# Experts in column strips: plain fp32 matmuls without a weight split, room for 96 rows an item, seven weight buffers

## The reference

```python
def swiglu(h, w_g, w_u, w_d):
    return (jax.nn.silu(h @ w_g) * (h @ w_u)) @ w_d

def moe_swiglu(h, w_router, w_g, w_u, w_d):
    t = h.reshape(-1, D_MODEL)
    logits = (t @ w_router).astype(jnp.float32)
    top_v, top_i = lax.top_k(logits, TOP_K)            # TOP_K = 2
    top_w = jax.nn.softmax(top_v, axis=-1)
    gate = jnp.sum(jax.nn.one_hot(top_i, N_EXPERTS, dtype=jnp.float32) * top_w[..., None], axis=1)
    for e in range(N_EXPERTS):                          # 8
        out = out + gate[:, e:e + 1] * swiglu(t, w_g[e], w_u[e], w_d[e])
```

## Time and profile before

| | before |
|---|---|
| median of 3 runs | 1993.19 us (1988.62 to 1993.28) |
| profiled execution | 1991.17 us |
| its span (first to last instruction) | 1989.4 us |
| mean granted clock of PE | 0.975 of full |
| PE busy | 1855.9 us (93%) |
| DVE busy | 1404.4 us (71%) |
| ACT busy | 1136.1 us (57%) |
| HBM read | 521.81 MB, 263 GB/s over the span |

### The profile page before, as it was taken

One profiled execution on the slowest core, in us unless ns is written; L12 is line 12 of the kernel. 1 busy time (PEld: TensorE's weight loads), 2 busy tenths in 40 slices (PEclk: granted clock), 3 DMA queues, 4 the chain that ended last, 5 costly groups with the idle time before them and its releaser, 6 DMA issues.

```text
span 1989.4 us, 28834 instructions
## 1 busy us (share of the span) xinstructions
PE 1855.9 (93%) x10925; PEld 1581.4 (79%) x10925; DVE 1404.4 (71%) x1711; ACT 1136.1 (57%) x1391; POOL 91.9 (5%) x105
## 2 busy tenths in 40 slices
PE   4999998999978899988999999999999999999997
PEld 2799888888866799986777777787777777777776
DVE  1477575434425577757888888888888788788885
ACT  2455544333323445525777767767777777777774
POOL 3010031000000100210000000000000000000000
PEclk8999998999998999988999999999999999999998
DMA  9364674677673444434989988989899899898993
GB/s 323 108 218 170 223 272 139 243 254 254 245 263 126 165 138 168 148 110 144 358 324 329 359 327 323 359 298 350 329 329 350 335 325 351 302 355 328 330 351 127
DMA packets 229738, 524.62 MB, mean 264 GB/s; under 512 B 5156, under 2 KB 11506, under 8 KB 229664
## 3 DMA queue, kind: packets, MB, share of 16 engines
q1 hardware_dynamic: 227456, 519.72, 72.5%
q0 software_dynamic: 2208, 3.85, 0.8%
HBM read 521.81 MB, written 1.74 MB: 263 GB/s over the span
## 4 chain that ended last, share of the span: by engine, by line
PE 60%; DVE 16%; DMA 9%; ACT 7%; issue 6%; POOL 1%; ACTq 0%; DVEq 0%; SPq 0%; POOLq 0%
PE ps L1380 18%; PE ps L1382 16%; PE ps L1381 16%; DVE wlo L1335 9%; ACT whi L807 4%; DMA raw<-in_w_ff_down_dram 3%; PE ps L1386 3%; DMA raw<-in_w_e_gate_dram 2%; DMA raw<-in_w_e_down_dram 2%; DVE wlo L857 2%; PE ps L1753 2%; PE ps L1441 1%; DMA raw<-in_w_ada_dram 1%; ACT whi L545 1%; PE ps L1775 1%
## 5 line engine op out<-in xcount | busy, mean ns | idle before, releaser
L1335 DVE TENSOR_TENSOR wlo<-raw,whi 128x1024 fp32r<-128x1024 f32 x672 | 780.5, 1220 | 115.2 <-ACT whi L807 115.2
L807 ACT ACTIVATE whi<-raw 128x1024 fp32r<-128x1024 f32 x672 | 669.4, 1053 | 38.8 <-PE ps L1382 38.7
L1380 PE MATMUL ps<-whi,hT_hi 128*128 128x512 f32 (+2 forms) x1024 | 407.6, 398 | 30.8 <-DVE wlo L1335 12.1
L857 DVE TENSOR_TENSOR wlo<-raw,whi 128x1024 fp32r<-128x1024 f32 (+1 forms) x220 | 266.8, 1247 | 218.2 <-ACT whi L545 218.0
L1381 PE MATMUL ps<-wlo,hT_hi 128*128 128x512 f32 (+2 forms) x1024 | 393.3, 384 | 0.0
L1382 PE MATMUL ps<-whi,hT_lo 128*128 128x512 f32 (+2 forms) x1024 | 392.8, 384 | 0.0
L1380 PE MATMUL ps<-hT_hi,whi 128*128 128x256 f32 x1248 | 361.6, 290 | 19.6 <-DVE hT_lo L902 8.4
L1381 PE MATMUL ps<-hT_lo,whi 128*128 128x256 f32 x1248 | 355.6, 285 | 0.0
L1382 PE MATMUL ps<-hT_hi,wlo 128*128 128x256 f32 x1248 | 355.4, 285 | 0.0
L545 ACT ACTIVATE whi<-raw 128x1024 fp32r<-128x1024 f32 (+1 forms) x220 | 222.0, 1049 | 119.3 <-PE ps L1382 45.6
L1380 PEld LDWEIGHTS ps<-whi,hT_hi 128*128 128x128 f32 x1024 | 194.0, 189 | 102.7 <-DVE wlo L1335 50.4
(11 more groups left out here) (269 smaller groups left out, 1779.7 us busy)
## 6 DMA issues: line engine op xcount, KB each, us to landing
raw<-in_w_e_gate_dram SPq DMA_DIRECT2D x56, 2048.0 KB, 7.8
raw<-in_w_e_up_dram SPq DMA_DIRECT2D x56, 2048.0 KB, 7.8
raw<-in_w_e_down_dram SPq DMA_DIRECT2D x56, 2048.0 KB, 7.7
raw<-in_w_ada_dram SPq DMA_DIRECT2D x24, 2048.0 KB, 10.6
raw<-in_w_in_dram SPq DMA_DIRECT2D x22, 2048.0 KB, 9.0
raw<-in_w_ff_gate_dram SPq DMA_DIRECT2D x7, 2048.0 KB, 7.7
raw<-in_w_ff_up_dram SPq DMA_DIRECT2D x7, 2048.0 KB, 7.9
raw<-in_w_ff_down_dram SPq DMA_DIRECT2D x7, 2048.0 KB, 8.1
```

Of the source, the lines that this page charges most:

```text
L807: act.activation(h, part, ACT.Copy).then_inc(hi_piece, 1)
L857: tt(w, part, h.bitcast(F32), ALU.subtract).then_inc(lo_piece, 1)
L1335: tt(w, part, h.bitcast(F32), ALU.subtract).then_inc(lo_piece, 1)
L1380: mm(out, a_hi, b_hi, start=start, stop=False, skip_group_check=shared)
```

## The change

The dense part stays as it is, but for the place of its tiles in SBUF. The four arrays `whi`, `wlo`, `acts_hi` (once `hT_hi` and `br_hi`) and `acts_lo` are given back after it, and four more weight buffers (`e_raw`) lie there. So the experts have seven buffers (E_SLOTS), the three of `raw` and these four.

In an item there is no split. The gathered tokens (`xe`) and the turned hidden tile (`hidT`) are plain fp32, and PE reads the weights where the DMA put them. An item has room for 96 rows (CAP = 96). Its tokens are the stationary operand in strips of 32: three strips hold the three groups of 32 tokens for one k-tile. The fourth strip does another share of the same chunk: the last four k-tiles of up for each group in turn (`UP_PARTS`), and in down the k-tiles 2 and 3 of the second output half (`Y_PARTS`). Its sums stand in partitions 96 to 127 of three banks. ACT moves each to its group's rows (`moved`), and DVE adds them.

With 96 rows a second level is needed: an expert may need two extra items (LEVELS = 2), and the table, its constants (now loaded by POOL behind the router's weights, `rconsts`) and the number of possible items grow (OVER from 3 to 5). The count alone is written first (`count_done`), so that PE and ACT need not wait for the whole table. Up is loaded ahead of gate.

```diff
-CAP = 128
+CAP = 96
+LEVELS = 2
 OVER = 512 // (CAP + 1)
...
+E_SLOTS = 7
+E_LOADS = [("up", 0), ("gate", 0)]
+for _c in range(1, CHUNKS):
+    E_LOADS += [("up", _c), ("gate", _c), ("down", _c - 1)]
+E_LOADS.append(("down", CHUNKS - 1))
...
+        e_raw = sb("e_raw", [P, E_SLOTS - RAW, 2 * HALF])
...
+            def given_back(j, i):
+                kind, ch = E_LOADS[j]
+                if kind == "down":
+                    sp.wait_ge(down_done, i * CHUNKS + (ch + 1))
+                else:
+                    sp.wait_ge(gu_done, i * (3 * CHUNKS) + (3 * ch + (3 if kind == "up" else 2)))
...
+                    if j >= E_SLOTS:
+                        given_back(j - E_SLOTS, i)
+                    elif not first:
+                        given_back(j - E_SLOTS + len(E_LOADS), i - 1)
+                    elif j < RAW:
+                        s = len(SLOTS) - RAW + j
+                        sp.wait_ge(lo_piece, 2 * (FIRST_HALF[s] + SLOTS[s][3]))
+                    elif j == RAW:
+                        sp.wait_ge(piece_used, 2 * HALVES)
...
+            pool.dma_start(rconsts, shape_consts[:, K_KEPT:K_COLS]).then_inc(router_in, 16)
...
+            def moved(dst, t, bank):
+                return act.activation(dst[32 * t:32 * t + 32, :], ps[CAP:P, bank, :], ACT.Copy)
             with act.Fori(0, n_items) as i:
-                        act.activation(h, part, ACT.Copy).then_inc(hi_piece, 1)
...
+                for ch in range(CHUNKS):
+                    for t in range(3):
+                        act.wait_ge(gu_done, i * (3 * CHUNKS) + (3 * ch + t + 1))
+                        if t == 1:
+                            act.activation(e_gate, ps[0:CAP, B_GATE, :], ACT.Silu)
+                        ins = moved(up_part, t, UP_PARTS[t])
+                    ins.then_inc(up_parted, 1)
+                    if ch == CHUNKS - 1:
+                        keep_gathered(i + 2)
+                    act.wait_ge(e_turn, i * CHUNKS + (ch + 1))
+                    act.activation(hidT[:, ch % 2, :, :].rearrange("p k s -> p (k s)"), ps[:, B_TURN, 0:4 * CAP],
+                                   ACT.Copy).then_inc(e_kept, 1)
...
+                act.wait_ge(down_done, i * CHUNKS + CHUNKS)
+                for t in range(3):
+                    moved(y_part, t, Y_PARTS[t])
+                act.activation(y_tok[:, 0:512], ps[0:CAP, B_Y, :], ACT.Copy).then_inc(y_parted, 1)
...
             with dve.Fori(0, n_items) as i:
-                        tt(w, part, h.bitcast(F32), ALU.subtract).then_inc(lo_piece, 1)
...
+                for ch in range(CHUNKS):
+                    dve.wait_ge(up_parted, i * CHUNKS + (ch + 1))
+                    tt(e_hidden, ps[0:CAP, B_UP, :], up_part, ALU.add).then_inc(up_sum, 1)
+                    dve.wait_ge(up_sum, i * CHUNKS + (ch + 1))
+                    tt(e_hidden, e_hidden, e_gate, ALU.mult).then_inc(e_hid, 1)
...
+            def gate_up(ch, i):
+                wu = landed("up", ch, i)
+                wg = landed("gate", ch, i)
+                for r in range(12):
+                    if r == 8 and ch:
+                        pe.wait_ge(e_kept, i * CHUNKS + ch)
+                    for t in range(3):
+                        if r < 8:
+                            mm(strip(B_GATE, t), tokens(r, t), wg[:, r, :], start=(r == 0), stop=(r == 7))
+                        else:
+                            mm(strip(B_UP, t), tokens(r - 8, t), wu[:, r - 8, :], start=(r == 8), stop=(r == 11))
+                    t, k = divmod(r, 4)
+                    ins = mm(strip(UP_PARTS[t], 3), tokens(4 + k, t), wu[:, 4 + k, :], start=(k == 0), stop=(k == 3))
+                    if k == 3:
+                        ins.then_inc(gu_done, 1)
...
+            def down(ch, i):
+                pe.wait_ge(e_kept, i * CHUNKS + (ch + 1))
+                wd = landed("down", ch, i)
...
+                for r in range(6):
+                    n, k = divmod(r, 4)
+                    if r == 4 and not last:
+                        turn_hidden(ch + 1, i)
+                    for t in range(3):
+                        mm(strip(B_Y + n, t), hidden(k, t), wd[:, k, 512 * n:512 * n + 512],
+                           start=first and k == 0, stop=last and k == (1 if n else 3))
+                    t, k = divmod(r, 2)
+                    ins = mm(strip(Y_PARTS[t], 3), hidden(2 + k, t), wd[:, 2 + k, 512:1024],
+                             start=first and k == 0, stop=last and k == 1)
+                ins.then_inc(down_done, 1)
...
             with pe.Fori(0, n_items) as i:
+                pe.wait_ge(xe_kept, i + 1)
+                for ch in range(CHUNKS):
+                    gate_up(ch, i)
+                    if ch == 0:
+                        scatter(i)
+                        turn_hidden(0, i)
+                    else:
+                        if ch == CHUNKS - 1:
+                            pe.wait_ge(selT_kept, i + 2)
+                            gather(i + 2)
+                        down(ch - 1, i)
+                down(CHUNKS - 1, i)
+            scatter(n_items)
```

More of the change, by code:

```diff
@@ L352, in piece_views @@
                 k, w, part = 1, 1024, whole[:, n:n + 1, :]
-            elif kind in ("tok", "na_qk") or item:
+            elif kind in ("tok", "na_qk"):
                 k, w, part = 2, width, whole[:, 2 * n:2 * n + 2, :]
@@ L357, in piece_views, with e_load @@
             return (part,) + tuple(x[:, buf, 0:k * w].rearrange("p (k n) -> p k n", k=k) for x in (whi, wlo))
[L359 to L367, removed]
-            return piece_views(kind, 0, hh % 2, c_, (len(SLOTS) + hh // 2) % RAW,
-                               (2 * (HALVES + hh) + c_) % PIECES, item=True)
+        def e_load(kind, ch):
+            j = E_LOADS.index((kind, ch))
+            k = 4 if kind == "down" else 8
+            return j, e_slot[j % E_SLOTS].rearrange("p (k n) -> p k n", k=k)
         def filled(l, f):
@@ L1765, in scatter, with strip, landed @@
-            def scatter(hh, i):
-                for r, bank in I_SCATTER[hh]:
-                    if r == 0:
-                        pe.wait_ge(y_kept, i + 1)
-                        pe.wait_ge(selT_kept, i + 1)
-                    if r == 3:
-                        pe.wait_ge(item_added, i * 4 + 1)
+            def strip(bank, t):
+                return ps[32 * t:32 * t + 32, bank, :]
+            def landed(kind, ch, i):
+                j, w = e_load(kind, ch)
+                pe.wait_ge(e_landed[j % E_SLOTS], i * (16 * len(E_LOADS) // E_SLOTS) + 16 * (j // E_SLOTS + 1))
+                return w
@@ new lines, in turn_hidden, with hidden @@
+            def turn_hidden(ch, i):
+                pe.wait_ge(e_hid, i * CHUNKS + (ch + 1))
+                for k in range(4):
+                    ins = turn(ps[:, B_TURN, CAP * k:CAP * k + CAP], e_hidden[:, P * k:P * k + P])
+                ins.then_inc(e_turn, 1)
+            def down(ch, i):
+                pe.wait_ge(e_kept, i * CHUNKS + (ch + 1))
+                wd = landed("down", ch, i)
+                first, last = ch == 0, ch == CHUNKS - 1
+                def hidden(k, t):
+                    return hidT[:, ch % 2, k, 32 * t:32 * t + 32]
+                if first:
+                    pe.wait_ge(item_added, i * 4 + 4)
+                for r in range(6):
[9 more added lines that the diff above has]
+                ins.then_inc(down_done, 1)
@@ L1773, in scatter @@
+            def scatter(i):
+                pe.wait_ge(y_kept, i + 1)
+                pe.wait_ge(selT_kept, i + 1)
+                for r in range(4):
                     for jj in range(2):
                         j = 2 * r + jj
-                        ins = mm(ps[:, bank, NT * jj:NT * jj + NT], y_tok[:, P * j:P * j + P], selT, start=True,
-                                 stop=True)
+                        ins = mm(ps[:, SCATTER_BANKS[r], NT * jj:NT * jj + NT], y_tok[:, P * j:P * j + P], selT,
+                                 start=True, stop=True)
```

316 lines of the change are left out of this document (118 added, 198 removed).

## The result

The changed kernel takes 2065.3 us (median of 4 runs, 2061.72 to 2068.94), the kernel before 1991.81 us in the same comparison. The ratio is 1.0371, 95% interval 1.0348 to 1.0395: 3.7% slower. 2032 was forecast; 2065.3 lies in the range, 33 us above the point. The profiled execution took 2061.72 us for a span of 2059.9.

The account below looks back on a forecast made before the run. PE was taken as the bound, with little slack in DMA. Start 914.4, nine items of 121.5 and end 20.8 gave a span of 2028.7 us, 2032 as median; range 2010 to 2088, chance 0.80.

Parts of the forecast that it names:

- Nine items: Expert stage: expert 0's 111 tokens exceed 96, so nine items run in place of eight, the ninth at full cost, 121.5 us.
- Strips, 108.4 us an item: PE in gate, up and down: 126 rounds of four strips at 0.86 us each, against 114.2 us for the split form.
- Turns, gather, scatter: PE's other work in an item: seven hidden-tile turns 4.6 us, gather 3.1, scatter 3.4, select-matrix turns 0.3.
- Left-over waits and drains: PE's remaining idle time in an item, shown by no row: between 0 and 6.9 us, taken as 1.7.
- DVE, ACT and the handoff: Item: DVE some 15 us, ACT some 25, neither bounds; 2.0 us handoff before PE's turn hidden with 1.4 to spare.
- DMA: Expert weight loads: 5.78 us each at 363 GB/s, ending at 1983 us, before PE's 2008, so costing nothing.
- one of the signs: Expected observation in the expert stage's profile: DMA share above 0.95.
- The late-load rival: Expert stage: late loads at 340 GB/s cost 45 us; with late handoffs 2060 to 2110 us, joint chance 0.16.
- Start, 914.4: Expert stage's first item starts at 914.4 us, with 2 us added for late router weights and constants, 2 for low clock.
- the 2 us for a low clock: Stage start: first matmuls run at 1.2 GHz after the sparse selection, adding 2 us.
- End: After the last item: three strip copies, one copy and an add replace one copy, 20.8 us in place of 18.7.
- Sum: Whole kernel: 914.4 + 9 x 121.5 + 20.8 = 2028.7 us span, 2030.5 profiled, 2032 as median.

Follow-up runs that it names:

- e2: Changed kernel with an extra item only above 128 tokens, so no ninth item and 15 tokens of expert 0 left out: 1940.39 us, ratio 0.9746.
- e9: Kernel before with items of 96 rows in place of 128, so nine items, weight split kept: 2125.05 us, ratio 1.0654.
- e1: Changed kernel with PE's first seven items written out and the last two in a loop, one taken jump left: 2027.88 us, ratio 1.0183.
- e12: Changed kernel with PE's items written out, expert 0's item with 128 rows, no ninth item: 1937.05 us, ratio 0.9710 against the kernel before.
- e5: Changed kernel with six rounds of each chunk's gate and up left out, all loads kept, 1530 instructions between jumps: 1926.25 us.
- e7: Kernel before with gate and up matmuls cut into two of 256 columns, 1936 instructions in the body: 2043.08 us.
- e8: Kernel before with gate, up and down matmuls cut into two of 256 columns, 2272 instructions in the body: 2057.34 us.
- e11: Changed kernel with three weight buffers in place of seven: 2603.88 us.
- e10: Changed kernel with expert loads after the first item's bringing only 32 columns, PE working on stale weights: 2029.65 us.

## Why the prediction was right on the sign and low by 33 us

- **Nine items**: right, and it decides the sign. e2 and e9 price it alone, 125 us with strips and 132 without.
- **Strips, 108.4 us an item**: right. Passes start 0.43 us apart throughout at full clock, and 500.00 of 500 us are busy where no jump lies (e1, e12).
- **Turns, gather, scatter**: forecast 4.6 + 0.3, 3.1 and 3.4 us. In the item from 1160.90 to 1286.60 us, groups by line (busy, mean ns):

```profile
L1396 PE MATMUL ps<-consts,big 96*128 96x96 f32 (+1 forms) x30 | 4.2, 259 | 0.0
L1763 PE MATMUL ps<-big 128*128 128x96 f32 x32 | 3.8, 277 | 0.0
L1841 PE MATMUL ps<-big 96*128 96x256 f32 x16 | 3.7, 386 | 0.0
```

  The gather costs what it did with 128 columns: its upper bound was the right one. The three make 11.7 us, and 11.4 had been put down for them. One reading behind them was wrong: the 0.21 us that I took for a drain between tiling modes is the length of a pass (0.63 us long, started 0.43 apart), with no switch near it. A switch from strips to the scatter costs 0.14 us here, the scatter starting 0.57 us after the last pass:

```profile
1048.80 0.63 PE L1798 MATMUL ps<-raw,KTt 128*32 128x512 f32 x3
...
1049.37 3.72 PE L1841 MATMUL ps<-big 96*128 96x256 f32 x16
```

- **The step that failed: "Left-over waits and drains", 1.7 us.** I looked there for waits on data. Within an item next to nothing is left: 120.33 us an item without a jump (e12), 0.2 more than strips and the three groups above, and 1.2 below the forecast. What I left out was no wait on data but the loop's own jump: 125.74 - 120.33 = 5.4 us at each of eight boundaries, 43.5 us in all. Its 0.2 us stood in the trace of before, as a row of the sequencer, and I took for granted that a longer body does not change it. The text on the change counted matmuls, four for a round in place of three for a k-tile, but priced only their time on the array.
- **DVE, ACT and the handoff**: right. No turn waits for `e_hid` in the stage.
- **DMA**: hidden, as forecast, but priced too high at 363 GB/s. Windows of 10 us show more:

```profile
1100.00:1110.00 10.00, 10.00 (x96) 2.99 (x92) 0.00 (x0) 2.21 (x4) 0.00 (x0) 1.00 1.04 402
```

  and e5 held 394 GB/s. The readings of the earlier trace rows were what three buffers asked for, not what DMA can do. It is also why one of the signs did not come: the DMA share of an item is 0.94, where I wanted it above 0.95. The Trainium skill (DMA: Bandwidth & Descriptors, Specifications) gives about 358 GB/s as a core's limit, one of two equal shares of a stack's 716; here one core loads alone, the 402 and 394 are above that share, and the measurement decides. The late-load rival rested on 340 and had less for it than I gave.
- **Start, 914.4**: 913.00 in the trace. PE does wait for the table constants, and starts the router at 888.47 in place of 885.90, 2.6 us late where I had put down 2; 1.1 of them come from upstream (POOL's memset at 878.88 in place of 877.79), so the constants cost less than I thought. And the 2 us for a low clock did not come, as the first strips run at full clock:

```profile
888.47 1.88 PE L1739 MATMUL ps<-qk,big 128*128 128x8 f32 x8 [6.20 <-DMA qk<-in_shape_consts_dram]
...
913.00 0.63 PE L1796 MATMUL ps<-raw,KTt 128*32 128x512 f32 x3 [0.87 <-ACT KTt L829]
...
913.42 0.63 PE L1796 MATMUL ps<-raw,KTt 128*32 128x512 f32 x3
```

- **End**: 20.8 us from the end of the last strip (2039.1) to the end of the span, as forecast.
- **Sum**: 2032, less 1.4 (start), less 9 x 1.2 (items), plus 43.5 (jumps), plus 1.6 (the median stands 3.6 over the profiled run, 2.0 before) is 2064.9, and 2065.3 was measured.

The 43.5 us of the jumps are a term from outside the forecast. That the time ended in the range is luck: the range had been opened for late handoffs and loads, of which there are none.

What stays open: where between 1530 and 1754 instructions the edge lies and why there; why most jumps of e7 and e8 are shorter than 6.2 us beside the same stream of weights (e11 has three buffers too, and its jumps take 6.2 us); and why the clock stayed up after one stop of 3.88 us. That in the changed kernel the stream lengthens the fetch is shown, by which resource they share is not.

## What to carry to other kernels

Count the instructions between a loop's jumps when an edit splits matmuls into smaller ones: even where they take the array no longer, the longer body may have to be fetched again at each jump. Read the taken branch on the sequencer's row, before and after, and write the loop out, or shorten the body, where it is long. And price a smaller tile by the worst count that the data has: 96 rows against 111 tokens cost a whole item here, and one wider item for that expert gave it back.

## What the runs showed of the hardware that was not expected

- A taken jump on PE takes 0.2 us with up to 1530 instructions between jumps, and 3.3 to 6.7 us with 1754 or more. In the changed kernel it is 3.4 us (median) with 20 GB/s on the DMA engines and 6.2 with 351; in e7 and e8 it is 4.0 to 6.0 us with the engines as busy. About 2.2 us of 6.2 are hidden, because the sequencer runs ahead of the array. Written-out code of eight items showed no stop (e12).
- After seven of the eight stops of 3.9 to 4.1 us the strips run at 1.2 GHz for some five passes, after one of 3.88 us they don't; after the eight stops of 1.1 to 1.7 us in e10 they never do.
- DMA brought 394 GB/s over 500 us with seven buffers waiting, where three had shown 362 to 367 in full windows.
- 32 gather matmuls take 3.8 us with 96 columns and 3.73 with 128.
